# A block of three float32 layers on one core: weight columns read from two halves 2 KB apart, and a reordered start

## The reference

```python
h = x + gla_mixer(rmsnorm(x))            # gated linear attention: 4 heads, chunks of 64 tokens
h = h + relu(rmsnorm(h) @ w_up)**2 @ w_down     # 2048 -> 8192 -> 2048
h = rmsnorm(h) * final_norm
# second block, on the normed h
proj = rmsnorm(h) @ w_in_2               # q, k, v, gate, x_lru, g_lru: 2048 -> 6144
y = concat(stick_breaking_attention(q, k, v) * silu(g),  rg_lru(conv(x_lru)) * silu(g_lru))
out = h + y @ w_out_2                    # 2048 -> 2048
```

## Time and profile before

| | |
|---|---|
| median of three runs | 1503.52 us |
| the profiled execution | 1504.49 us |
| its span, from the first to the last instruction | 1502.7 us |
| PE busy | 1494.1 us (99%) |
| DVE busy | 854.3 us (57%) |
| ACT busy | 719.4 us (48%) |
| mean busy share of the DMA engines, first fortieth of the span | 9 tenths, 328 GB/s |
| the same, over the whole span | 186 GB/s |
| granted TensorE clock, mean | 0.998 of full |

### The profile page before, as it was taken

One profiled execution on the slowest core, in us unless ns is written; L12 is line 12 of the kernel. 1 busy time (PEld: TensorE's weight loads), 2 busy tenths in 40 slices (PEclk: granted clock), 3 DMA queues, 4 the chain that ended last, 5 costly groups with the idle time before them and its releaser, 6 DMA issues. The chain is left out here.

```text
span 1502.7 us, 17691 instructions
## 1 busy us (share of the span) xinstructions
PE 1494.1 (99%) x7210; PEld 1252.8 (83%) x7210; DVE 854.3 (57%) x889; ACT 719.4 (48%) x858; POOL 23.8 (2%) x44
## 2 busy tenths in 40 slices
PE   8999999999999999999999999999999999999999
PEld 7788888888888888888888888888888888888887
DVE  5555545555556545655555655565656776565654
ACT  5543544445544433444344433444554664565632
POOL 1000000000000000000000000000000011000000
PEclk9999999999999999999999999999999999999999
DMA  9444465557555555555555555555555455544563
GB/s 328 151 157 163 144 198 179 184 179 240 188 187 187 196 190 189 191 186 196 194 184 196 185 194 196 186 192 189 186 173 180 155 194 189 165 152 159 183 221 124
DMA packets 77760, 279.16 MB, mean 186 GB/s; under 512 B 8704, under 2 KB 9216, under 8 KB 77296
## 3 DMA queue, kind: packets, MB, share of 16 engines
q1 hardware_dynamic: 75744, 273.06, 54.5%
q0 software_dynamic: 784, 3.08, 0.7%
q10 hardware_dynamic: 1152, 1.90, 0.4%
HBM read 275.91 MB, written 2.10 MB: 185 GB/s over the span
## 5 line engine op out<-in xcount | busy, mean ns | idle before, releaser
L1006 DVE TENSOR_TENSOR w_lo<-raw,w_hi 128x1024 fp32r<-128x1024 f32 x508 | 620.5, 1225 | 601.0 <-ACT w_hi L709 599.8
L709 ACT ACTIVATE w_hi<-raw 128x1024 fp32r<-128x1024 f32 x508 | 536.8, 1059 | 720.2 <-PE banks L403 503.4
L401 PE MATMUL banks<-w_hi,xa 128*128 128x512 f32 x752 | 301.1, 400 | 0.5 <-DVE w_lo L1006 0.5
L401 PE MATMUL banks<-w_hi,xb 128*128 128x512 f32 x768 | 299.6, 390 | 0.0
L403 PE MATMUL banks<-w_hi,xb 128*128 128x512 f32 x768 | 298.9, 389 | 0.0
L402 PE MATMUL banks<-w_lo,xb 128*128 128x512 f32 x768 | 298.8, 389 | 0.0
L403 PE MATMUL banks<-w_hi,xa 128*128 128x512 f32 x752 | 294.3, 391 | 0.0
L402 PE MATMUL banks<-w_lo,xa 128*128 128x512 f32 x752 | 294.1, 391 | 0.0
L425 PE MATMUL banks<-xa,w_hi 128*128 128x512 f32 x1024 | 256.4, 392 | 0.0
L425 PEld LDWEIGHTS banks<-xa,w_hi 128*128 128x128 f32 x1024 | 184.4, 189 | 33.1
L403 PEld LDWEIGHTS banks<-w_hi,xb 128*128 128x128 f32 x768 | 144.2, 188 | 29.9
(11 more groups left out here) (196 smaller groups left out, 612.8 us busy)
## 6 DMA issues: line engine op xcount, KB each, us to landing
raw<-in_weights SPq DMA_DIRECT2D x511, 512.0 KB, 3.3
h<-in_x SPq DMA_DIRECT2D x2, 1024.0 KB, 11.6
arena<-in_x_turned SPq DMA_DIRECT2D x7, 256.0 KB, 6.5
result<-stage ACTq DMA_DIRECT2D x6, 256.0 KB, 4.5
arena<-in_final_norm POOLq DMA_DIRECT2D x1, 1024.0 KB, 7.6
raw<-in_weights SPq DMA_DIRECT2D x2, 256.0 KB, 4.1
arena<-in_gla_b_gate POOLq DMA_DIRECT2D x1, 512.0 KB, 9.3
arena<-in_lru_w_a POOLq DMA_DIRECT2D x1, 512.0 KB, 10.0
```

Of the source, the lines that this page charges most:

```text
L401: pe.matmul(o, xh[:, kt, xs], w_hi[:, slot, k, :], start=kt == 0, stop=False)
L709: act.activation(w_hi[:, n % RING, :, :], raw[:, n % RING, :, :], ACT.Copy)\
L1006: dve.tensor_tensor(w_lo[:, n % RING, :, :], raw[:, n % RING, :, :], w_hi[:, n % RING, :, :].bitcast(F32), ALU.subtract).then_inc(lo_ready, 1)
```

## The change

1. In 48 panels the host lays a chunk out anew: the even columns of both groups come first (512 values per partition, 256 for each group), then the odd columns. In a partition an even column and the odd one beside it are then 512 x 4 bytes = 2 KB apart. The matmuls read them through a view that takes one value of each half in turn, so that the columns arrive in their old order. The up panels keep their layout.
2. The first chunk's two parts are now cut across both halves, 2 x 256 values per partition where it was 512 in a row.
3. ACT issues the parameters (`par`) before the first piece of x_turned.
4. SP issues the residual's x two chunks later.
5. 26 transposes instead of 34 go ahead of the first matmul.

```diff
+        def woven(w, slot, k):
+            return w[:, slot, :, k * S:(k + 1) * S].rearrange("p a b -> p b a")
...
-            sp.dma_start(raw[:, 0, 0, :], weights[0, :, 0, :]).then_inc(first_in, 16)
-            sp.dma_start(raw[:, 0, 1, :], weights[0, :, 1, :]).then_inc(raw_in[0], 16)
+            for k, arrived in ((0, first_in), (1, raw_in[0])):
+                sp.dma_start(raw[:, 0, :, k * S:(k + 1) * S], weights[0, :, :, k * S:(k + 1) * S]).then_inc(arrived, 16)
...
+            load(CH)
+            load(CH + 1)
             for tt in range(TT):
+                load(CH + 2 + tt)
                 sp.dma_start(h[:, tt, :], x_v[:, tt, :]).then_inc(x_in[tt], 16)
-                load(CH + tt)
-            for n in range(CH + TT, CH * PANELS):
+            for n in range(CH + 2 + TT, CH * PANELS):
                 load(n)
...
-                pe.matmul(o, xh[:, kt, xs], w_hi[:, slot, k, :], start=kt == 0, stop=False)
-                pe.matmul(o, xh[:, kt, xs], w_lo[:, slot, k, :], start=False, stop=False)
-                return pe.matmul(o, xl[:, kt, xs], w_hi[:, slot, k, :], start=False, stop=kt == KT - 1)
+                pe.matmul(o, xh[:, kt, xs], woven(w_hi, slot, k), start=kt == 0, stop=False)
+                pe.matmul(o, xh[:, kt, xs], woven(w_lo, slot, k), start=False, stop=False)
+                return pe.matmul(o, xl[:, kt, xs], woven(w_hi, slot, k), start=False, stop=kt == KT - 1)
...
-            keep_running(34)
+            keep_running(26)
...
+            act.dma_start(par[:, :], columns).then_inc(par_in, 16)
             act.dma_start(x_t[:, 0:CK, :], x_turned[:, 0:CK, :]).then_inc(xt_in[0], 16)
-            act.dma_start(par[:, :], columns).then_inc(par_in, 16)
...
-                act.activation(w_hi[:, 0, k, :], raw[:, 0, k, :], ACT.Copy).then_inc(done, 1)
+                own = slice(k * S, (k + 1) * S)
+                act.activation(w_hi[:, 0, :, own], raw[:, 0, :, own], ACT.Copy).then_inc(done, 1)
...
+    def woven(w, first, count):
+        chunks = panels(w, first, count)
+        return chunks.reshape(-1, P, CK, N // 2, 2).transpose(0, 1, 4, 2, 3).reshape(-1, P, 2, CK * N // 2)
+
...
-    parts.append(panels(a["gla_w_out"][0], 0, 4))
+    parts.append(woven(a["gla_w_out"][0], 0, 4))
     for b in range(MLP_BLOCKS):
         parts.append(panels(a["mlp_w_up"][0], b * D, 4))
-        parts.append(panels(a["mlp_w_down"][0][b * D:(b + 1) * D], 0, 4))
+        parts.append(woven(a["mlp_w_down"][0][b * D:(b + 1) * D], 0, 4))
```

More of the change, by code:

```diff
@@ L437, in multiply_first @@
                         for tt in range(TT):
-                            last = pe.matmul(acc(0, tt), xs[:, kt, tt * P:(tt + 1) * P], ws[:, 0, kt, :],
+                            last = pe.matmul(acc(0, tt), xs[:, kt, tt * P:(tt + 1) * P], woven(ws, 0, kt),
                                              start=kt == 0 and ws is w_hi and xs is xa_hi, stop=False)
@@ L453, in multiply_next @@
                         for tt in range(TT):
-                            last = pe.matmul(acc(0, tt), xs[:, kt, tt * P:(tt + 1) * P], ws[:, c, k, :],
+                            last = pe.matmul(acc(0, tt), xs[:, kt, tt * P:(tt + 1) * P], woven(ws, c, k),
                                              start=False, stop=False)
@@ L1427, in _ @@
                 dve.wait_ge(rounded, 1)
-                dve.tensor_tensor(w_lo[:, 0, k, :], raw[:, 0, k, :], w_hi[:, 0, k, :].bitcast(F32), ALU.subtract)\
-                    .then_inc(done, 1)
+                own = slice(k * S, (k + 1) * S)
+                dve.tensor_tensor(w_lo[:, 0, :, own], raw[:, 0, :, own], w_hi[:, 0, :, own].bitcast(F32),
+                                  ALU.subtract).then_inc(done, 1)
             for n in range(1, RING):
@@ L1448, in panels @@
         return w.transpose(0, 4, 1, 3, 2, 5).reshape(-1, P, CK, N)
+    def woven(w, first, count):
+        chunks = panels(w, first, count)
+        return chunks.reshape(-1, P, CK, N // 2, 2).transpose(0, 1, 4, 2, 3).reshape(-1, P, 2, CK * N // 2)
     gla_in, in_2 = a["gla_w_in"][0], a["w_in_2"][0]
     keys_at, vals_at, gates_at = GH * GDK, 2 * GH * GDK, 2 * GH * GDK + D
-    parts = [panels(gla_in, keys_at, 2), panels(gla_in, 0, 2)]
+    parts = [woven(gla_in, keys_at, 2), woven(gla_in, 0, 2)]
     for j in range(GH):
-        parts += [panels(gla_in, vals_at + j * N, 1), panels(gla_in, gates_at + j * N, 1)]
-    parts.append(panels(a["gla_w_out"][0], 0, 4))
+        parts += [woven(gla_in, vals_at + j * N, 1), woven(gla_in, gates_at + j * N, 1)]
+    parts.append(woven(a["gla_w_out"][0], 0, 4))
     for b in range(MLP_BLOCKS):
         parts.append(panels(a["mlp_w_up"][0], b * D, 4))
-        parts.append(panels(a["mlp_w_down"][0][b * D:(b + 1) * D], 0, 4))
-    parts += [panels(in_2, first, 2) for first in (4096, 1024, 0, 2048, 3072, 5120)]
-    parts.append(panels(a["w_out_2"][0], 0, 4))
+        parts.append(woven(a["mlp_w_down"][0][b * D:(b + 1) * D], 0, 4))
+    parts += [woven(in_2, first, 2) for first in (4096, 1024, 0, 2048, 3072, 5120)]
+    parts.append(woven(a["w_out_2"][0], 0, 4))
     columns = np.concatenate([np.reshape(a[name], (-1, P)) for name in (
```

## The result

The changed kernel took 1458.97 us, median of 6 runs (1457.61 to 1459.70), against 1503.46 of 6 runs of the kernel before beside them: a ratio of 0.970, 95% interval 0.9685 to 0.9713. That is 44.5 us less where 54.5 were forecast, and inside the range of 1436 to 1501. The profiled span fell from 1502.7 to 1457.6 us, by 45.1.

The account below looks back on a forecast made before the run. The prediction took PE's matmul pace, 226.7 ns each, as the bound. Its terms, 52.4 + 0.9 + 2.8 + 0.9 - 1.5 - 1.0 = 54.5 us less, took the 1502.7 us span to 1448.2, forecast 1449, range 1436 to 1501.

Parts of the forecast that it names:

- What bounds the kernel: PE, busy 99% of the span: its weight matmuls start every 226.7 ns, where 512 columns need 213.3 at full clock.
- The pace of a woven matmul: Weight matmuls outside the up panels: 215.3 ns instead of 226.7 for 4593 of them, 52.4 us less.
- two regions: Reason for the woven pace: memory regions 2 KB apart, each asked every second cycle, show no loss; 215.3 ns.
- no loss is left: Assumption for woven weight matmuls: the extra cycle per 16 columns goes wholly, leaving 213.3 ns plus a fixed 2 ns.
- The rule of the Trainium skill: Rival on woven reads: a new 16-byte line at each access costs, 1561 to 2419 us in all; slower given 0.13.
- The start: Before PE's first weight matmul: parameters issued first let it start at 7.0 to 7.1 us, 0.9 us less.
- The residual's x: Waits at gate_up: the first matmul's goes, 2.8 us less; the third's grows from 0.7 to 2.3 us, 1.5 back.
- The halved clock: Stretch at half clock from 38.4 to 41.8 us, costing 1.7 us: half a chance to go, 0.9 us less.
- Work at its own pace: Small chains between panels on ACT and DVE don't shorten with PE, so some gain is lost: 1.0 us more.

Follow-up runs that it names:

- kernel of patterns: Kernels of matmuls alone, each executed once, stepping through the moving side in many ways; fp32r took 226.9 ns contiguous, 215.8 alternating by one value.
- the residual's x in one go: On top of the whole change, both parts of the residual's x go out together behind chunk 10, ahead of chunk 11; 1456.70 us, ratio 0.9685.
- The kernel in which PE never waits there: On top of the residual's x in one go, gate_up's second half moved behind one more chunk of matmuls; 1451.40 us, ratio 0.9654.

## Why the prediction was right, and where it wasn't

*What bounds the kernel* was right. The start-to-start distances of the matmuls of L401 to L403 sum to 1050.0 us before and 1001.7 after, with some new waits among them: 48.4 us, more than the net 45.1; all else together lost some. That the view is the cause of the gain is shown by the kernel that has it alone.

*The pace of a woven matmul*, 215.3 ns taken and 215.8 measured, is the term that carries the result. Its value came from the excess of 32 cycles in 544, its absence at the halved clock, and the fixed 2 ns of plain fp32 matmuls. The reason given for it was wrong: no two regions are needed, since halves 16 bytes apart do as well. The number stood on "no loss is left", and that held for a reason that these runs don't give; as far as it hung on the two regions, it came out by luck, and bf16 and ordinary fp32 show how easily the same step could have cost time.

*The rule of the Trainium skill* that spoke against the change ("Advanced Engine Details and Errata", section "SBUF Cachelines": two accesses in a row to a 16-byte line, or a penalty) doesn't hold for fp32r values in two alternating streams, and the trace decides: 215.8 ns. It fits other rows of the same kernel of patterns: every 16th column 433 ns, and bf16 in alternation 484 instead of 216. It doesn't fit fp32r in every second column, which takes two values of each such line and yet 450.6 ns.

*The start* failed as a step: 0.9 us forecast, 0.3 measured. I let par's landing move ahead and left x_turned's where it was, though it is issued 0.4 us later for it and is four times as large. ACT then waited for that (6.36). Of the start's time a single profile tells little: the granted clock rose to full at 7.6 us before and at 6.4 after, but already at 4.9 in the kernel with the view alone, which was through with its 34 transposes and at its first weight matmul at 6.85 us.

*The residual's x* failed in its second half. The first wait went as worked out (the copy ran at 31.05, PE asked at 32.7). Its successor was named and placed, but sized at 2.3 us in all; it is 4.3. Of the chain, h's landing was put at 32 and was 35.1, because its second part stood on SP behind chunk 11's load, which was issued only at 25.3, when DVE had split chunk 7. From the timelines of DVE and SP:

```profile
24.09 1.23 DVE L1012 TENSOR_TENSOR w_lo<-raw,w_hi 128x1024 fp32r<-128x1024 f32 x1 [1.39 <-ACT w_hi L714]
25.34 0.33 SPq L277 DMA_DIRECT2D raw<-in_weights  x1
25.71 0.98 SPq L293 DMA_DIRECT2D h<-in_x  x1
```

I had counted bytes ahead of it and not that wait on SP. (SP's load of chunk n waits for the split of chunk n - 4, the last user of its slot; the n - 3 in the description of the kernel before, and the chunk 8 in the expectation for the residual's x in one go, are one too high.)

*The halved clock* is the largest miss, 4.3 us. I gave the stretch from 38.4 us on half a chance to go and didn't look at the other one, from 69.1 us on. The first came back at the new wait, for twice as long, and the second grew with it. The kernel in which PE never waits there has neither in its profile, but two of its other three runs had a mean granted clock of 0.997; so what sets these stretches stays open, and the half chance rested on one of them following a wait.

*Work at its own pace*, 1.0 us forecast, 1.1 measured: DVE's scan chain in the second block holds PE for 0.6 and 1.1 us.

## What to carry to other kernels

Compare the distance from start to start of the limiting matmul with its columns over the clock, at both clock levels: an excess in proportion to the columns that is gone at 1.2 GHz points to how the moving side is read, and other orders of reading are worth a measurement, for each type by itself, since what gained 5% for fp32r more than doubled bf16. Before a transfer is moved back, follow the second consumer's chain to its end, with every wait of the queue that issues it; and where PE waits for some us, look at what the clock loses behind it too, over several runs, and see whether the next piece of PE's own work can go ahead of the waiting one.

## What was not expected of the hardware

- fp32r, 512 columns: 226.9 ns contiguous, 215.8 in two alternating streams at any distance from 16 B to 8 KB, 236.9 contiguous from an odd column on, 450.6 in every second column.
- bf16: 216 contiguous, 484 in two alternating streams; ordinary fp32, one record: 429 contiguous and 540 in alternation.
- In the profiled executions the granted clock fell to half near 70 us in all kernels that had waited for 2.8 us or more between 33 and 45 us, and didn't in the one that hadn't waited; those with woven up panels, with 0.3 to 0.7 us of wait there, had one such stretch of 6.8 us, near 64 us. Other executions of the kernel without the wait had a mean granted clock of 0.997, so the rule isn't general. What ties the two places together wasn't tried.
